# The stream's squares at two stage boundaries: five VectorE additions against ones-matrix products between TensorE's blocks

## What is computed

```python
def _rms_norm(x, g):
    xf = x.astype(jnp.float32)
    y = xf * lax.rsqrt(jnp.mean(xf * xf, axis=-1, keepdims=True) + RMS_EPS)
    return (y * g.astype(jnp.float32)).astype(x.dtype)

for i in range(DEPTH):                       # 0: RWKV-7, 1: latent attention
    u = _rms_norm(h, norm_pre[i])
    m = mixer_i(u)
    h = h + _rms_norm(m, norm_post[i])
x = h[:, N_META:]
x = x + short_conv_fourier_mixer(rms_norm(x, norm_even[0]), ...)   # u @ w_in first
```

## Time and profile before

| what | us |
|---|---|
| median of 3 runs | 2340.65 (2336.63 to 2343.60) |
| the profiled execution | 2341.08 |
| its span, from first to last instruction | 2339.3 |
| TensorE busy in it | 2137.1 (91%) |
| VectorE / ScalarE / GpSimd busy | 1272.9 / 826.9 / 1061.8 |
| mean granted TensorE clock | 0.965 |

### The profile page before, as it was taken

How to read it: one execution, slowest core, us unless ns; L and a number is a source line. 1 busy time by engine, 2 the same in 40 slices (tenths; PEclk the granted TensorE clock), 3 DMA queues, 4 the chain that set the end, 5 groups by cost and what they waited for, 6 DMA issues and landing times.

```text
span 2339.3 us, 57688 instructions
## 1 busy us (share of the span) xinstructions
PE 2137.1 (91%) x23340; PEld 1803.7 (77%) x23340; DVE 1272.9 (54%) x1984; ACT 826.9 (35%) x2170; POOL 1061.8 (45%) x651
## 2 busy tenths in 40 slices
PE   6799999988999999995979999999998899898997
PEld 4599888987888888884979956777688676676765
DVE  6656556654666666665346614444422575528664
ACT  1644444434655555554112122333311101102341
POOL 1133434323332332335875821222288598865445
PEclk8899999999999999996989999999989899999999
DMA  2234443455442343323212220110123231221102
GB/s 94 92 126 158 151 153 145 154 157 136 79 93 64 79 93 76 70 64 118 93 63 82 90 63 28 36 36 18 36 63 111 83 98 54 72 73 63 46 1 72
DMA packets 158977, 197.86 MB, mean 85 GB/s; under 512 B 121040, under 2 KB 123344, under 8 KB 156496
## 3 DMA queue, kind: packets, MB, share of 16 engines
q1 hardware_dynamic: 158800, 195.25, 28.2%
HBM read 156.24 MB, written 38.99 MB: 83 GB/s over the span
## 4 chain that ended last, share of the span: by engine, by line
PE 59%; issue 7%; POOL 4%; DVE 4%; ACT 2%; POOLq 1%; DVEq 0%; ACTq 0%
PE wide L1310 9%; PE wide L1311 9%; PE wide L1312 9%; PE wide L833 9%; PE wide L1855 5%; PE wide L1964 2%; PE wide L1743 2%; PE wide L1920 1%; PE wide L2540 1%; PE wide L1948 1%; PE wide L2220 1%; POOL x_w L1124 1%; PE wide L2523 1%; PE wide L858 1%; POOL n_levels L1118 1%
## 5 line engine op out<-in xcount | busy, mean ns | idle before, releaser
L1310 PE MATMUL wide<-mixed_high,w_high_rwkv_in 128*128 128x264 f32 x720 | 211.0, 293 | 16.4 <-issue 9.3
L1312 PE MATMUL wide<-mixed_high,w_low_rwkv_in 128*128 128x264 f32 x720 | 206.6, 287 | 0.0
L1124 POOL TENSOR_TENSOR x_w<-n,masks 128x192 f32<-128x192 f32 x48 | 28.7, 597 | 360.2 <-ACT n L1001 360.2
L564 POOL TENSOR_TENSOR w_low_rwkv_in<-weights,w_high_rwkv_in 128x1024 fp32r<-128x1024 f32 x45 | 107.7, 2406 | 174.5 <-ACT w_high_rwkv_in L439 174.5
L355 PE MATMUL wide<-mixed_in,weights 128*128 128x264 f32 x672 | 160.4, 397 | 12.4 <-DVE mixed_in L325 12.3
L1331 POOL TENSOR_TENSOR w_high<-weights,con 128x1024 fp32r<-128x1024 f32 x51 | 123.2, 2416 | 90.8 <-PE wide L1312 50.2
L355 PEld LDWEIGHTS wide<-mixed_in,weights 128*128 128x128 f32 x672 | 127.5, 193 | 44.9 <-issue 16.2
L1310 PEld LDWEIGHTS wide<-mixed_high,w_high_rwkv_in 128*128 128x128 f32 x720 | 138.0, 192 | 29.3 <-issue 27.4
L1312 PEld LDWEIGHTS wide<-mixed_high,w_low_rwkv_in 128*128 128x128 f32 x720 | 137.9, 192 | 0.0
L1334 POOL TENSOR_TENSOR w_low<-weights,w_high 128x1024 fp32r<-128x1024 f32 x51 | 134.8, 2644 | 4.0
L833 PE MATMUL wide<-x_w,n_levels 64*64 64x64 f32 x2752 | 121.0, 223 | 4.5 <-issue 0.6
(11 more groups left out here) (393 smaller groups left out, 6542.0 us busy)
## 6 DMA issues: line engine op xcount, KB each, us to landing
weights<-in_stream SPq DMA_DIRECT2D x200, 512.0 KB, 3.6
forms<-form SPq DMA_DIRECT2D x16, 2020.5 KB, 6.3
forms_in<-forms SPq DMA_DIRECT2D x96, 144.0 KB, 4.5
forms_in<-forms SPq DMA_DIRECT2D x32, 288.0 KB, 4.4
gate_bonus<-forms SPq DMA_DIRECT2D x16, 576.0 KB, 3.9
r_ahat_r<-forms SPq DMA_DIRECT2D x32, 144.0 KB, 3.5
mixed<-gate_bonus SPq DMA_DIRECT2D x14, 264.0 KB, 2.1
gated<-mixed SPq DMA_DIRECT2D x14, 264.0 KB, 4.7
```

Of the source, the lines that this page charges most:

```text
L564: pool.tensor_tensor(w_in[1][:, at, :], ring.slot(load), w_in[0][:, at, :].bitcast(F32), ALU.subtract).then_inc(w_split, 1)
L1310: pe.matmul(dst, w[0], x[0], start=start, stop=False)
L1312: return pe.matmul(dst, w[1], x[0], start=False, stop=stop)
```

## The change

TensorE takes over the whole sum. In pe_first, behind each block k from 1 on, stands now the product of ones with the squares of tile k-1 (pe_add_squares); the last one, of tile 7, stands behind them in pe_sum_updated and counts n_summed. VectorE's five additions go, at both boundaries. The order of VectorE's other work stays.

```diff
-        def pe_first(pe, load, rhs, width, parts):
+        def pe_first(pe, load, rhs, width, parts, summed=None):
...
                     if k == KD - 1:
                         mm.then_inc(ring.done(load + t), 1)
+                if summed and k >= 1:
+                    pe_add_squares(pe, k - 1, summed, width)
...
+        def pe_add_squares(pe, k, squares, width):
+
+            st = seen["pe"]
+            if k == 0:
+                pe.wait_ge(n_rooted, st.norms)
+            pe.wait_ge(sq_made, st.squares + k + 1)
+            for b in range(2 if width == L else 1):
+                n = HALF if width == L else width
+                mm = pe.matmul(sum_bank(3, width)[b], ones, squares(k)[:, b * n:(b + 1) * n], start=k == 0, stop=k == KD - 1)
+            return mm
+
+        def pe_sum_updated(pe, squares, width):
+
+            st = seen["pe"]
+            pe_add_squares(pe, KD - 1, squares, width).then_inc(n_summed, 1)
+            st.norms += 1
+            st.squares += KD
...
-            def add(k):
-                if 0 < k < SUMMED:
-                    dve_add_squares(dve, k, lambda n: wide_squares(n, width), width)
...
-                add(k - 2)
             dve.drain().then_inc(n_used, 1)
             dve_low(dve, KD - 1, gain, u_parts, width)
-            for k in range(KD - 2, SUMMED):
-                add(k)
...
         def pe_sum_mixer(pe, width):
-            pe_sum(pe, width, KD, SUMMED - 1, [sq_sum[:, 0:width]] + [wide_squares(k, width) for k in range(SUMMED, KD)], sum_bank(3, width))
+            pe_sum_updated(pe, lambda k: wide_squares(k, width), width)
...
-            pe_first(pe, MLA_IN, half_parts(u_mla), L, first_parts(MLA_IN, w_mla_first, w_parts))
+            pe_first(pe, MLA_IN, half_parts(u_mla), L, first_parts(MLA_IN, w_mla_first, w_parts),
+                     summed=lambda k: wide_squares(k, L))
...
-            pe_first(pe, load, whole_parts(u_even), SEQ, first_parts(load, w_even_first, w_parts2))
+            pe_first(pe, load, whole_parts(u_even), SEQ, first_parts(load, w_even_first, w_parts2),
+                     summed=lambda k: wide_squares(k, SEQ))
```

More of the change, by code:

```diff
@@ L1471, in act_project_mixer @@
             st.squares += KD
-            st.added += SUMMED - 1
             st.used += 1
```

## The result

The changed kernel takes 2349.20 us (median of 9 runs, 2343.54 to 2351.51) against 2336.63 us of before in the same comparison (9 runs, 2334.94 to 2343.82). The ratio is 1.0043, 95% interval 1.0028 to 1.0057: 10 us slower, between 6.5 and 13.3. The forecast was 2349.5. The median of before is 4 us lower here than in the three runs first shown, which are among the nine; in three later comparisons, of 35, 35 and 27 runs, it is 2340.83, 2341.64 and 2341.57. Where this scatter comes from is part of what follows.

The account below looks back on a forecast made before the run. TensorE, busy 91% of the span, was taken as the bound. First boundary +4.45 - 0.35 = +4.1, second +4.27 + 0.43 = +4.7, together +8.8 us on the median 2340.65: 2349.5 us, range 2345.5 to 2353.5.

Parts of the forecast that it names:

- The bound: Both boundaries: TensorE, busy 91% of the span, sets the time; without the adds it falls further behind VectorE each k.
- The adds' removal, 0.35 us at the first boundary and 0 at the second: Dropping VectorE's five adds per boundary gives back only TensorE's one wait for u_low, 0.35 us, at the first boundary.
- The price of a sum, 0.89 and 0.85 us: TensorE's float32 product per operand; five more per boundary, all on the path: +4.45 us at the first, +4.27 at the second.
- The weights: Weights behind block 7 released later: TensorE waits 0.43 us more at the second boundary; 0.5 us slack at the first, cost 0.
- The sum: Both boundaries together: +4.1 us at the first and +4.7 at the second, +8.8 us in all.
- The clock: Rival: the second boundary's low-clock stretch gets as short as the first's, giving back 1.4 us: +7.4, 2348.1 us; chance 0.12.
- a later stage whose length differs by more than 1 us: Sign named beforehand that would show the prediction wrong, beside sums spaced at 0.12 or TensorE waiting inside the blocks.
- The margin of 1 to 2 us: How far a median of three runs can be off; for it 0.13 of the forecast's 0.72 went to within 0.3%.

Follow-up runs that it names:

- adds_kept: The changed kernel with VectorE's five adds put back at both boundaries, their sum unread; 1.0029 (1.0018 to 1.0039) of before.
- no_adds: The kernel before without VectorE's five adds at both boundaries, only squares of tiles 5 to 7 summed (output not right); 0.9988 (0.9975 to 1.0000) of before.
- sums_behind: The changed kernel with all eight tiles of squares summed on TensorE behind the eighth block instead of between blocks; 1.0030 (1.0020 to 1.0041) of before.
- held pair of kernels: Kernel before and changed kernel, each with one wait added delaying GpSimd's split in the last attention's projection until VectorE's with_gain; means 2336.36 and 2345.00 us.
- before_gain_first: The kernel before with VectorE making the next head's with_gain ahead of the gate step in the last attention's projection; 0.9985 (0.9974 to 0.9997) of before.
- spectral_only: The change at the second boundary (spectral block) alone, the first boundary as in the kernel before; 1.0005 (0.9993 to 1.0018) of before.

## Why the prediction was right

**The bound.** Right. TensorE waits nowhere inside the blocks of the changed kernel, and adds_kept shows VectorE in its shadow.

**The adds' removal, 0.35 us at the first boundary and 0 at the second.** Right for an execution with low stretches of 3.2 and 6.1 us: no_adds gives 0.34 and -0.1. The step that was too narrow is the zero: with a shorter low stretch at the second boundary the adds cost up to 0.5 us there, and with a longer one at the first they cost nothing.

**The price of a sum, 0.89 and 0.85 us.** Right: four records in 0.89 us between products, and reciprocals 4.08 and 4.25 us later where 4.1 and 4.27 were worked out. The 131 ns per matmul of 512 columns that the Trainium skill gives ("TensorE: Matmul & The Clock Gate", section "Back-to-back issue gap") would have made it an estimated 1.3 us at the second boundary. The rows do not agree: a record of a float32 sum takes 0.43 us there, one of a float32r sum 0.23.

**The weights.** Right at the second boundary: 4.61 - 4.25 = 0.36 us for the 0.43 worked out, and gone in sums_behind. At the first boundary SyncE issued the load 4.97 us later against the first product (4.99 worked out), but GpSimd began 3.6 us behind the issue instead of 4.3, so only 4.2 us later. Its split ended at 1256.63, and TensorE came to that tile at 1252.08 + 48 x 0.12 = 1257.9: the slack was 1.2 us, not the 0.5 that I had. It changed nothing.

**The sum.** +8.8 us; the two boundaries of the profiles have 4.08 + 4.61 = 8.7, the held pair of kernels 8.6.

**The clock.** The rival was rightly sized for one stretch: low stretches at the first boundary of 3.2, 4.1 and 5.6 us stand in kernels whose instructions are the same up to there (before, before_gain_first, spectral_only), and 6.1 and 3.9 us at the second boundary (before, before_gain_first). The Trainium skill, "TensorE: Matmul & The Clock Gate", section "Part 1: The HAM clock gate", says that the number of slow matmuls at a start differs from run to run of the same kernel; these rows agree. What I missed is the term that matters more. I wrote that a later stage whose length differs by more than 1 us would show the prediction wrong, and one differed by 5.2 us. By that sign the prediction was wrong about this stage, in which it had no term. The stage took its two lengths in kernels with and without the change, on which of two engines came first by 0.2 us. The margin of 1 to 2 us that I gave a median of three runs was too small: it moved by 4 us with six more runs, and runs of before lie 9 to 15 us apart. That the median came out at 2349.2 for 2349.5 is in part luck: in that comparison the medians lie 12.6 us apart and the ratio makes it 10.0, where 8.8 were forecast.

**Open.** Whether the change shifts the share of the two lengths. spectral_only's runs (+1.2 us, at most 4.2) are below its 4.7, which such a shift would explain. An estimate takes the held kernels' means as those of the short rest (2336.36, and 4.65 more for spectral_only) and 5.3 us for the long one. By the means of the runs, the long rest then comes in about 0.8 of the runs of before (2340.73), 0.7 of the changed kernel's (2348.68 against 2345.00) and 0.3 of spectral_only's (2342.67 against 2341.0), each uncertain by some 0.4. This does not decide it. What moves the first boundary's start by up to 5.8 us, with the same instructions, is open too.

## What to carry to other kernels

When work moves from one engine to another, ask first which of the two is ahead, then what one operand costs in the form in which it will run: a ones-matrix product in float32 took 3.7 times as long as one in float32r (0.85 against 0.23 us), and the VectorE add that it replaced was hidden. Everything put ahead of the last product of a tile also delays what that product releases, so follow the load and the split behind it.

If runs of one kernel fall into groups, split the span at marks before looking at causes: one stage may have two lengths, and holding one of the two colliding engines can be worth more than many a change: here it gave 4.4 us, half of what the change under study cost.

## What the runs showed of the hardware

A GpSimd split that started 0.16 us ahead of VectorE's step stretched that step from 0.68 to 2.83 us and the following one from 0.48 to 2.56. TensorE waited 4.88 us for it, and executions with such a wait were 5.3 us longer. TensorE's clock stayed at the low one of its two levels (1.2 GHz, granted 0.50) for 2.8 to 6.0 us at the first boundary and 3.5 to 6.1 at the second, each time behind 12.9 to 13.0 us without products. A sum of 512 columns took 0.85 us in float32, as two records, and 0.23 us in float32r, as one.
